# Sample state update and merge in one block, with the products on u between the state steps

## What is computed

```python
def mixer_block(xn, conv_prev, h0, lp):
    ...
    y, h_new = ssd_scan(xs, dt, a, bm, cm, h0)
    y = y + lp['d_skip'].astype(jnp.float32)[:, None] * xs.astype(jnp.float32)
    y = gated_rmsnorm(y.reshape(bsz, L, SSM_D_INNER), z, lp['ssm_norm'])
    a_out = y @ lp['w_a_proj']
    ...
    b_out = spatial_gating(u, v, lp['gm_ws'], lp['gm_bs']) @ lp['w_b_proj']
    gates = jax.nn.sigmoid(xn @ lp['w_gate'] + lp['b_gate'])
    merged = gates[..., :D_MODEL] * a_out + gates[..., D_MODEL:] * b_out
    return merged @ lp['w_out'], conv_new, h_new, v
```

## Time and profile before

| | us |
|---|---|
| median of 3 runs (2147.55 to 2153.63) | 2147.64 |
| the execution that was profiled | 2150.74 |
| its span, from the first to the last instruction | 2148.9 |
| PE busy in it | 2035.4 (95%) |

### The profile page before, as it was taken

One profiled execution on the slowest core, in us unless ns is written; L12 is line 12 of the kernel. 1 busy time (PEld: TensorE's weight loads), 2 busy tenths in 40 slices (PEclk: granted clock), 3 DMA queues, 4 the chain that ended last, 5 costly groups with the idle time before them and its releaser, 6 DMA issues. The chain is left out here.

```text
span 2148.9 us, 32905 instructions
## 1 busy us (share of the span) xinstructions
PE 2035.4 (95%) x12276; PEld 1773.0 (83%) x12277; DVE 1029.4 (48%) x1140; ACT 774.3 (36%) x1099; POOL 375.4 (17%) x507
## 2 busy tenths in 40 slices
PE   7999999999999999789999999999899899999996
PEld 5778999999888888648998789877788788887884
DVE  4215245453556556344323341335543663785666
ACT  4322122222343434332002121423412254785675
POOL 2000100010444445320001000000000121122114
PEclk9999999999999999799999999999999999999998
DMA  5121232333343433593434311244403667898887
GB/s 192 61 85 65 70 99 79 88 89 89 93 132 105 130 107 98 143 302 105 146 101 163 128 59 39 99 166 157 149 30 150 222 202 257 297 372 299 289 289 289
DMA packets 243711, 324.29 MB, mean 151 GB/s; under 512 B 15838, under 2 KB 161790, under 8 KB 243570
## 3 DMA queue, kind: packets, MB, share of 16 engines
q1 hardware_dynamic: 207796, 267.60, 37.2%
q0 software_dynamic: 7344, 25.38, 4.6%
q10 hardware_dynamic: 28480, 30.02, 4.0%
HBM read 250.97 MB, written 73.28 MB: 151 GB/s over the span
## 5 line engine op out<-in xcount | busy, mean ns | idle before, releaser
L274 PE MATMUL psum<-hT_high,t_w_high 128*128 128x352 f32 x576 | 186.9, 324 | 0.3 <-DVE t_w_low L1016 0.3
L276 PE MATMUL psum<-hT_high,t_w_low 128*128 128x352 f32 x576 | 185.6, 322 | 0.0
L275 PE MATMUL psum<-hT_low,t_w_high 128*128 128x352 f32 x576 | 185.6, 322 | 0.0
L3669 ACT ACTIVATE e_w_high<-big 128x2048 fp32r<-128x2048 f32 x94 | 175.0, 1907 | 25.1 <-PEq L2807 17.2
L3796 DVE TENSOR_TENSOR e_w_low<-big,e_w_high 128x2048 fp32r<-128x2048 f32 x64 | 144.0, 2288 | 38.4 <-ACT e_w_high L3669 37.5
L3573 PE MATMUL psum<-e_w_high,e_xT_high 128*128 128x512 f32 x368 | 147.4, 401 | 5.0 <-DVE e_xT_low L3791 3.0
L3575 PE MATMUL psum<-e_w_high,e_xT_low 128*128 128x512 f32 x368 | 145.4, 395 | 0.0
L3574 PE MATMUL psum<-e_w_low,e_xT_high 128*128 128x512 f32 x368 | 145.4, 395 | 0.0
L274 PE MATMUL psum<-hT_high,s_w_high 128*128 128x352 f32 x384 | 132.1, 344 | 0.0
L276 PE MATMUL psum<-hT_high,s_w_low 128*128 128x352 f32 x384 | 124.9, 325 | 0.0
L275 PE MATMUL psum<-hT_low,s_w_high 128*128 128x352 f32 x384 | 124.8, 325 | 0.0
(11 more groups left out here) (553 smaller groups left out, 4858.3 us busy)
## 6 DMA issues: line engine op xcount, KB each, us to landing
big<-in_w_expert_gate SPq DMA_DIRECT2D x32, 1024.0 KB, 9.4
big<-in_w_expert_up SPq DMA_DIRECT2D x32, 1024.0 KB, 9.9
big<-in_w_expert_down SPq DMA_DIRECT2D x32, 1024.0 KB, 11.1
t_w<-in_w_in SPq DMA_DIRECT2D x24, 512.0 KB, 4.9
x_scr<-t_conv_out ACTq DMA_DIRECT2D x20, 512.0 KB, 4.5
gate_scr<-s_gate_tanh ACTq DMA_DIRECT2D x16, 528.0 KB, 3.3
m_gates<-gate_scr SPq DMA_DIRECT2D x16, 528.0 KB, 5.5
scan_w<-in_w_gate SPq DMA_DIRECT2D x16, 512.0 KB, 4.2
```

The costliest lines, as they stand in the source:

```text
L274: nc.tensor.matmul(out, ah, w_h, start=start, stop=False)
L275: nc.tensor.matmul(out, ah, w_l, start=False, stop=False)
L276: return nc.tensor.matmul(out, al, w_h, start=False, stop=stop)
L3669: return nc.scalar.activation(dst, src, ACT.Copy)
```

## The change

The two blocks become one, `stage_sample_merge`.

- The 24 products on `u` (8 model tiles x 3 slabs, called chunks, 12 matmuls each) are put among the 12 state steps: 18 of them by the list `IN_STEP`, 6 behind the last step. Each result is multiplied by its gate and stored back into `gate_scr`, in the place of the gate (`store_b`); the products on `y` load it from there later.
- The weights for `u` have their own two buffers. SP issues the load of tile f+1 when it comes to chunk 3f in its order, which is the last chunk of a step, behind that step's state store and state load. ACT splits them (`b_high`) between two copies of turned tiles (`copied`), DVE behind `b_gated` of the same chunk.
- The state tiles go in another order, and `yoff` runs once for every four: 32 matmuls of 128 columns, for four groups of 32 output rows in turn.
- `turn` has one PSUM place, so it waits for the copy of the tile before. The new state is added in place, in one of seven buffers.
- The loads of `y` are issued in the first burst. `u` is split ahead of the first copy of a turned tile. `y` is split behind the last step.
- The filler matmuls between the two blocks go. The products on `y` alternate between two sets of three PSUM banks, their weights are split in two halves.

```diff
+    RING, PT, GR, HK = 7, 3, 3, XF // 2
+    ORDER = [gg * PT + f for f in range(PT) for gg in range(G)]
+    IN_STEP = (1, 1, 2, 1, 2, 1, 2, 1, 2, 2, 1, 2)
...
+            def load_bw(f):
+                if f >= 2:
+                    sp.wait_ge(s_bwl, f - 1)
+                sp.dma_start(bw[:, f % 2], w_b[:, :, f * P:(f + 1) * P]).then_inc(s_bw[f % 2], 16)
...
+            def chunks_done(lo, hi):
+
+                for q in range(lo, hi):
+                    f = q // 3
+                    if q % 3 == 0 and 1 <= f < DK - 1:
+                        load_bw(f + 1)
+                    if q % 3 == 2:
+                        store_b(f)
+                        if 1 <= f and f + 2 < DK:
+                            load_gate(f + 2)
...
+            for i in range(XF):
+                chunks_done(first_chunk[i], first_chunk[i + 1] - 1)
+
+                sp.wait_ge(s_hn, i + 1)
+                sp.dma_start(h_out[ORDER[i]], h0[:, slot(i)]).then_inc(s_ho[slot(i)], 16)
+                if i >= 2 and i - 2 + RING < XF:
+                    sp.wait_ge(s_ho[slot(i - 2)], 16)
+                    load(i - 2 + RING)
+                chunks_done(first_chunk[i + 1] - 1, first_chunk[i + 1])
...
+            def turn(i):
+
+                pe.wait_ge(s_h0[slot(i)], 16 * (uses(i) + 1))
+                if i == 0:
                     pe.wait_ge(s_xd, 1)
                     pe.wait_ge(s_xt, 1)
                 else:
+                    pe.wait_ge(s_hc, i)
...
+                for b in range(NB):
+                    for gg in range(G):
+                        mm = nc.tensor.matmul(ps[gg * NS:(gg + 1) * NS, YO, f * P:(f + 1) * P], cm[:, b, gg, :], hT[:, gg, b, :],
+                                              start=(b == 0), stop=(b == NB - 1))
...
+            for i in range(XF):
+                for q in range(first_chunk[i], first_chunk[i + 1] - 1):
+                    chunk(q)
+                if i + 1 < XF:
+                    turn(i + 1)
+                state(i)
+                if i == 0:
+                    ydiag()
+                chunk(first_chunk[i + 1] - 1)
+                if i % G == G - 1:
+                    yoff(i // G)
...
+            def b_high(f):
+                act.wait_ge(s_bw[f % 2], 16 * (f // 2 + 1))
+                if f >= 2:
+                    act.wait_ge(s_bm, 3 * f - 3)
+                nc.scalar.activation(bwh[:, f % 2], bw[:, f % 2], ACT.Copy, scale=0.5).then_inc(s_bwh, 1)
...
+            b_high(0)
+            act.wait_ge(s_xs, 1)
+            act.wait_ge(s_bma, 1)
+            act.wait_ge(s_bmv, 1)
+            for t in range(GMF):
+                nc.scalar.activation(uh[:, t], g.uT[:, t], ACT.Copy).then_inc(s_uh, 1)
+            b_high(1)
+            for i in range(XF):
+                copied(i)
+                for q in range(first_chunk[i], first_chunk[i + 1]):
+                    if q % 3 == 0 and q:
+                        b_high(q // 3 + 1)
...
+                stt(gb[f % GR][:, x], gb[f % GR][:, x], 1.0, ps[:, BB + q % 2, 0:SLAB], ALU.add, ALU.mult).then_inc(s_bg, 1)
+                if n == 0 and 1 <= f < DK - 1:
+                    b_low(f + 1)
...
-            g.keep_busy(6, 12)
-            product(0, 0, lambda k: pe.wait_ge(s_sl, k + 1))
-            product(1, 1, lambda k: pe.wait_ge(s_sl, GMF + k + 1))
```

More of the change, by code:

```diff
@@ L1576, in stage_ssd_sample @@
         cf = g.sb("q_part_signs", [P, 4], ctx=ctx)
[L1577 to L1580, removed]
         ss = g.sb("q_ss", [P, 1], ctx=ctx)
@@ L1607, in _ @@
             for gg in range(G):
                 sp.dma_start(zin[gg * NS:(gg + 1) * NS, :], g.z_scr[c][0:NS, gg * XW:(gg + 1) * XW]).then_inc(s_z, 16)
-            for q in range(2):
[L1610 to L1620, removed]
+            load_gate(0)
@@ new lines, in _ @@
+            load_y(0)
+            for i in range(4, RING):
+                load(i)
+            load_gate(1)
+            load_y(1)
+            load_gate(2)
+            load_y(2)
+            for i in range(XF):
[6 more added lines that the diff above has]
+                chunks_done(first_chunk[i + 1] - 1, first_chunk[i + 1])
@@ new lines, in _ @@
+            gates(0)
+            sp.wait_ge(s_ad, 1)
+            gates(1)
+            query_w(sp, s_qw)
+            with sp.Fori(2, DK) as f:
+                for k in range(2):
+                    sp.wait_ge(s_wl, (f - 1) * 2 + k + 1)
+                    load_a(f, k)
+                sp.wait_ge(s_ad, f)
+                gates(f)
+            for i in range(XF):
+                sp.wait_ge(s_ho[slot(i)], 16 * (uses(i) + 1))
+            sp.wait_ge(s_qw, 64)
+            for s in range(2):
+                sp.wait_ge(s_mst[s], 16 * (DK // 2))
@@ L1718, in ydiag, with chunk @@
                 mm.then_inc(s_yd, 1)
-            turn(0)
[L1721 to L1725, removed]
-                    ydiag()
-                if u % PT == PT - 1:
-                    yoff(u // PT)
+            def chunk(q):
+                f, n = q // 3, q % 3
+                if n == 0:
+                    pe.wait_ge(s_bwl, f + 1)
+                if q == 0:
+                    pe.wait_ge(s_bs, 1)
+                    pe.wait_ge(s_bh, 1)
+                if q >= 2:
+                    pe.wait_ge(s_bg, q - 1)
+                x = slice(n * SLAB, (n + 1) * SLAB)
+                for k in range(GMF):
+                    if q == 0:
+                        pe.wait_ge(s_ul, k + 1)
+                    mm = matmul3(nc, ps[:, BB + q % 2, 0:SLAB], bwh[:, f % 2, k, :], bwl[:, f % 2, k, :],
+                                 uh[:, k, x], ul[:, k, x], k == 0, k == GMF - 1)
+                mm.then_inc(s_bm, 1)
@@ new lines, in _, with w_high @@
+            b_high(1)
+            for i in range(XF):
+                copied(i)
+                for q in range(first_chunk[i], first_chunk[i + 1]):
+                    if q % 3 == 0 and q:
+                        b_high(q // 3 + 1)
+            for f in range(first_chunk[XF] // 3, DK - 1):
+                b_high(f + 1)
+            def w_high(f, k, to):
+                act.wait_ge(s_w[k], f * 16 + 16)
+                nc.scalar.activation(to[:, half(k)], wa[:, half(k)], ACT.Copy, scale=0.5).then_inc(s_wh, 1)
@@ new lines, in _, with tile @@
+            w_high(0, 0, wh0)
+            for i in range(5, XF - 2):
+                act.wait_ge(s_ho[slot(i)], 16 * (uses(i) + 1))
+            for t in range(7, 10):
+                y_high(t)
+            act.wait_ge(s_ys, 1)
+            nc.scalar.activation(yh[:, :, SEQ:T], g.yT[:, :, SEQ:T], ACT.Copy).then_inc(s_sh, 1)
+            w_high(0, 1, wh0)
+            for t in range(10, XF):
+                y_high(t)
+            act.wait_ge(s_bm, CHUNKS)
+            def tile(f, s, more, waits):
+                if more:
+                    for k in range(2):
+                        if waits:
+                            act.wait_ge(s_mh, f * 2 + k + 1)
+                        w_high(f + 1, k, wh)
+                act.wait_ge(s_ad, f + 1)
+                act.dma_start(g.merged_scr[f], mo[:, s, :]).then_inc(s_mst[s], 16)
@@ L1762, in _ @@
+            tile(0, 0, True, False)
+            with act.Fori(0, DK // 2 - 1) as i:
+                for s in range(2):
+                    tile(i * 2 + 1 + s, 1 - s, True, True)
+            tile(DK - 1, 1, False, False)
         @block.vector
@@ new lines, in _, with w_low @@
+            y_low(5)
+            def w_low(f, k, to):
+                dve.wait_ge(s_wh, f * 2 + k + 1)
+                stt(to[1][:, half(k)], wa[:, half(k)], 0.5, to[0][:, half(k)].bitcast(F32), ALU.mult, ALU.subtract).then_inc(s_wl, 1)
+            w_low(0, 0, (wh0, wl0))
+            b_gated(next(left))
+            for t in range(6, 10):
+                y_low(t)
+            dve.wait_ge(s_sh, 1)
+            tt(yl[:, :, SEQ:T], g.yT[:, :, SEQ:T], yh[:, :, SEQ:T].bitcast(F32), ALU.subtract).then_inc(s_sl, 1)
@@ new lines, in _, with gated, following @@
+            w_low(0, 1, (wh0, wl0))
+            for t in range(10, XF):
+                y_low(t)
+            def gated(f, banks):
+                dve.wait_ge(s_mh, f * 2 + 2)
+                dve.wait_ge(s_gt, f * 32 + 32)
+                stt(slabs(gt[:, 0, :]), slabs(gt[:, 0, :]), 1.0, ps[:, banks:banks + 3, 0:SLAB], ALU.add, ALU.mult).then_inc(s_pr, 1)
+            def following(f):
+                for k in range(2):
+                    w_low(f + 1, k, (wh, wl))
+            following(0)
@@ L2012, in stage_out_query @@
+            gated(0, 0)
+            with dve.Fori(0, DK // 2 - 1) as i:
+                for s in range(2):
+                    following(i * 2 + 1 + s)
+                    gated(i * 2 + 1 + s, 3 - 3 * s)
+            gated(DK - 1, 3)
 def stage_out_query(g, x, x_dram, w, qT, qT_at, kv_at, mem):
```

440 lines of the change are left out of this document (219 added, 221 removed).

## The result

The changed kernel takes 2172.3 us (median of 4 runs, 2169.97 to 2173.46) where the kernel before, run beside it, took 2148.69 (4 runs): a ratio of 1.0103, interval 1.0088 to 1.0117. It is slower by about 23 us; the prediction was 2169. The profiled execution took 2169.97, its span is 2168.2.

A forecast was written before the change was run, and what follows sets the result against it. PE was taken to set the time in the merge and to wait in the state steps. Terms of -32.6 (work), +38.7 (waits) and +15 (clock) gave +21 us on the 2147.64 median, 2169 us; range 2154 to 2182.

The forecast's parts named there:

- The work without waits: Joined block, PE with no new waits: last product ends at 1121.8 against 1154.4, 32.6 us less.
- The bound for groups in series: State steps: the yoff groups would take 21 us in all if their matmuls ran in series, against 7.0 assumed.
- The waits: Joined block: PE waits for late weights of u and at the first and third products on y, 38.7 us more.
- The sixth: Wait before chunk 21: tile 7's load is issued at chunk 18, b_low(7) stands before b_gated(19); 3 us.
- The landing of 6.0: Weights of u: each 256 KB load lands in 6.0 us, bounded by 4.4 and 8.7, with other transfers in front.
- The clock: Behind PE's pauses: half clock costs about 3 us at four long ones, perhaps half at two; 15 us, bounds 0 and 18.
- DMA: Joined block: the transfer volume costs nothing, 12 us where landings go to 8.7; the way through DRAM is hidden.
- rival C: Joined block: the DMA queue sets the pace, landings go to 8.7 us; +16, 2185 us; chance 0.12 together with D.
- A: Rival, joined block: the weights come quickly and the kernel gets faster; priced at -12, 2136 us; chance 0.14.
- B: Rival, joined block: waits as summed, clock holds, landings at the short end; 0 to +6, about 2150 us; chance 0.12.
- D: Rival, state steps: yoff runs in series; +14, 2183 us; chance 0.12 together with C.

The follow-up runs named there:

- e1: The changed kernel with the load of the weights of u for tile f+2 issued where chunk 3f is done, three chunks sooner; 2127.75 us, ratio 0.9899 to before.
- e7: The changed kernel with the u weights loaded three chunks sooner and stores of the gated u product cut to 16 of 128 rows; 2142.03 us, block 242.9 us.
- e4: The changed kernel with the weight load ahead of the state store and state load in steps ending with a tile's first chunk; 2159.96 us, ratio 1.0040 to before.
- e2: The changed kernel with 30 filler matmuls on PE ahead of each of turns 4, 6 and 8; 2169.02 us, ratio 1.0093 to before.

## Why the prediction was right, point by point

*The work without waits* (-32.6 us). e1 has it nearly pure: its block is 28.9 shorter than before. Take the 5.1 us of waits ahead of its first and third products on `y` off, and it would be 34. The new start came a little sooner than I had it (`turn(1)` 26.4 us behind the first matmul in the changed kernel, 27.5 predicted), and the `yoff` groups took 1.95 each, not 2.3. Against that, the half clock at the start lasted for 9.4 us of PE's work, not 6, which is 1.7 us more. The bound for groups in series falls.

*The waits* (38.7 us). Measured, in the order of the prediction: 7.66, 8.37, 8.41, 4.40, 2.70, 6.11 us between the chunks (predicted 8.4, 8.8, 8.8, 4.5, 2.6, 3), 0.74 at the start of the first product on `y` (0.9), 2.79 ahead of the third (1.7): 41.2. The last of these came as predicted, for weights issued behind the four loads of `w_out`:

```profile
1051.24 2.80 SPq L4166 DMA_DIRECT2D v_w<-in_w_out  x4
1054.40 3.43 SPq L1679 DMA_DIRECT2D m_w<-in_w_a_proj  x2
...
1066.56 0.43 PE L274 MATMUL psum<-yT_high,m_w_high 128*128 128x352 f32 x1 [2.79 <-DVE m_w_low L2120]
```

The first five are right to 0.8 us. The sixth, before chunk 21, was twice its size, and it is the term that was mis-sized. SP issued that load only at 1010.60, behind a store and a gate load whose issue alone took 2.42 us, and behind the split DVE still had a low part of `y` (1.2 us) and the mean of the squares (1.3 with its wait) ahead of `b_gated(19)`. I had not written that chain out as I did the others. The landing of 6.0 that carried the term was 5.9 in the median; from issue to split it was 5.6, 6.3 and 6.3 us ahead of the three long pauses.

*The clock* (15 us). It is what is left between the changed kernel and e1: 291.3 - 243.3 = 48.0, less the difference of the waits, 41.2 - 5.1 = 36.1, makes 11.9 us. The trace has it directly as well. These are the stretches of half clock behind the pauses of 7.66, 8.37, 8.41, 4.40 and 6.11 us (length, then PE's busy time):

```profile
925.38:935.62 10.24, 5.01 (x19) 4.84 (x20) 1.91 (x2) 1.53 (x2) 1.90 (x1) 0.50 0.28 77
945.86:956.10 10.24, 4.09 (x16) 3.92 (x17) 1.91 (x2) 2.54 (x3) 1.90 (x1) 0.50 0.41 116
966.34:976.58 10.24, 5.63 (x21) 5.47 (x22) 1.92 (x2) 1.53 (x2) 1.90 (x1) 0.50 0.30 84
990.23:993.64 3.41, 3.08 (x12) 2.91 (x13) 0.69 (x3) 1.20 (x2) 0.99 (x1) 0.50 0.02 5
1017.54:1024.36 6.82, 4.64 (x17) 4.60 (x18) 5.64 (x10) 5.21 (x7) 0.55 (x1) 0.50 0.29 84
```

PE worked 22.4 us in them, half of which, 11.2, is the loss; e1 has no such stretch between the start and the end of its block. So the remainder is the clock. I had three full falls, the fourth also full, and two halves. In the trace five of the pauses, from 4.40 us up, brought the clock down, for 1.5 to 2.8 us each, and the one of 2.70 us did not: the clock was 1.00 around it. The two errors (2.5 more in waits, 3 less in clock) cancel.

*DMA* (nothing). Right where it was claimed, by e7 and by the 319 GB/s of e1 with PE fully busy. The 8.7 us landings of rival C did not come: the six late loads took 4.4 to 6.3 us from issue to split.

*The rivals.* A (the weights land fast enough) needed a landing of 2.5 us; the shortest was 4.4, and even with nothing of the step in front (e4) 3.1. Its sums were loose: with a landing of 2.5 us and the clock falling in the long pauses only, its own terms give -32.6 + (38.7 - 21) + 9 = -6, not -8, and nothing there supports the -12 that it was priced at. In the same way B's terms begin at 2148, not at the 2146 that the range was drawn from. B needed the clock to hold; it fell at the pauses of 4.40 us and more. D is refuted by the 1.95 us groups.

*By the Trainium skill.* The page "DMA: Bandwidth & Descriptors", section "Anatomy of one DMA — SWDGE (gpsimd) path", has a fixed 2.0 us and the bytes at 436 GB/s, by which, as an estimate, 256 KB would take 2.6. The weights landed in 4.4 us at best and 5.9 in the median in the changed kernel, and in 3.1 at best and 4.4 in the median in e4; the fit is for the gpsimd path, while these loads are issued by SP, and no run here shows a plain load on that path. What stood in front in the same queue made about half of the difference (e4). The Trainium skill's page "TensorE: Matmul & The Clock Gate", section "HAM oscillation — how this bites in real kernels", describes a loop that waits for a DMA in each round and starts each on the throttled clock. The trace agrees for the five pauses of 4.40 us and more, and not for the one of 2.70. The 18 us that the prediction has as the upper bound, all six in full, were not reached.

*What was luck.* The block grew by 19.1 us where 21 was forecast: -33.9, 41.2 and 11.9 in place of -32.6, 38.7 and 15, so the errors of the three terms, 1.3, 2.5 and 3.1 us, went partly against each other. The medians grew by 23.6; the difference to the block is the spread of the executions, which no step of mine touches.

## What to carry to other kernels

When work is put into the gaps of another loop, follow the loads of the work that is put in: where in the queue each is issued, and what stands behind the instruction that waits for it on its engine. Here the joined block without late loads was worth 29 us, and one load of 256 KB in every third chunk, issued three chunks too late, cost 48. A load belongs where its buffer comes free, not where the loop happens to come past. And a wait of PE of 4 us or more is to be priced with the slow work behind it: here 1.5 to 2.8 us each. Of the shorter ones some cost as much and some nothing, so two kernels whose blocks differ by 1 or 2 us are not told apart by one profile each.

## What was not expected of the hardware

Short pauses go either way. In e2 one of 2.05 us was followed by some 3 us at the half clock, one of 2.08 was not. In e1 and e4 the pause ahead of the third product on `y` is 3.07 us in both; the clock held in e1 and fell in e4, for 3.4 us of work:

```profile
1018.35 0.43 PE L274 MATMUL psum<-yT_high,m_w_high 128*128 128x352 f32 x1 [3.07 <-DVE m_w_low L2120]
...
1021.00:1024.00 3.00, 3.00 (x21) 3.00 (x20) 0.00 (x0) 0.00 (x0) 2.27 (x1) 1.00 0.00 0
```

```profile
1052.75 0.43 PE L274 MATMUL psum<-yT_high,m_w_high 128*128 128x352 f32 x1 [3.07 <-DVE m_w_low L2123]
...
1054.00:1057.00 3.00, 3.00 (x12) 3.00 (x12) 1.14 (x1) 0.00 (x0) 1.78 (x1) 0.50 0.00 0
```

In the changed kernel the clock held through 2.70 us; the stretches around that pause:

```profile
1003.00:1005.00 2.00, 0.04 (x1) 0.00 (x0) 0.19 (x1) 0.85 (x2) 0.00 (x0) 1.00 0.20 60
...
1006.00:1010.00 4.00, 4.00 (x79) 3.80 (x68) 3.64 (x6) 0.00 (x0) 0.00 (x0) 1.00 0.52 151
```

Matmuls onto 32 rows, issued for four groups of rows in turn, ran at 1.95 us for 64 records, 0.030 each, where a record in one group of rows took 0.33 for 384 columns, so 0.11 for 128 as an estimate. The earlier rows of this shape, 0.043 and 0.036, had a half-clock part and a tail in them.
